# Delta rule's heads: a 16-column slab's TensorE passes set between those of the slab behind it

## The reference

```
proj = u @ w_in
dn_qkv, dn_z, dn_b, dn_a, ... = jnp.split(proj, idx, axis=-1)
qkv = jax.nn.silu(causal_depthwise_conv(dn_qkv, conv_w))
q, k, v = jnp.split(qkv, 3, axis=-1)          # q and k are then l2-normed by head
beta = jax.nn.sigmoid(dn_b)
g = -jnp.exp(a_log) * jax.nn.softplus(dn_a + dt_bias)
o_a = gated_delta_rule(q, k, v, g, beta)
```

## Time and profile before

| | |
|---|---|
| time, median of 3 runs | 3174.45 us (3172.67 to 3175.84) |
| profiled execution, its own time | 3191.96 us |
| its span, first to last instruction | 3190.7 us |
| mean granted clock of TensorE | 0.952 of full |
| PE busy | 3049.1 us (96%) |
| DVE, ACT, POOL busy | 2014.7, 1233.4, 340.1 us |

### The profile page before, as it was taken

One profiled execution on the slowest core, in us unless ns is written; L12 is line 12 of the kernel. 1 busy time (PEld: TensorE's weight loads), 2 busy tenths in 40 slices (PEclk: granted clock), 3 DMA queues, 4 the chain that ended last, 5 costly groups with the idle time before them and its releaser, 6 DMA issues.

```text
span 3190.7 us, 55249 instructions
## 1 busy us (share of the span) xinstructions
PE 3049.1 (96%) x23638; PEld 2868.9 (90%) x23638; DVE 2014.7 (63%) x2878; ACT 1233.4 (39%) x1633; POOL 340.1 (11%) x331
## 2 busy tenths in 40 slices
PE   7999998999998799998999999999999999999999
PEld 4888887999998677998999989889999998997998
DVE  4576586777786577677656854566565576446654
ACT  2222223545443133433544421445454443134643
POOL 5000001101010122002100020011020102000201
PEclk9999998999998799898998989999999999999999
DMA  7243244799996566797655612346576663232664
GB/s 262 95 151 127 89 156 116 204 258 270 262 280 196 160 210 201 202 257 215 180 164 151 168 54 67 100 131 180 169 197 168 168 160 92 65 96 69 191 168 129
DMA packets 746224, 524.76 MB, mean 164 GB/s; under 512 B 19242, under 2 KB 711660, under 8 KB 745852
## 3 DMA queue, kind: packets, MB, share of 16 engines
q1 hardware_dynamic: 741852, 516.18, 56.4%
q0 software_dynamic: 4128, 5.06, 0.5%
HBM read 520.07 MB, written 2.94 MB: 164 GB/s over the span
## 4 chain that ended last, share of the span: by engine, by line
PE 79%; DVE 9%; ACT 5%; issue 5%; DMA 2%; SPq 0%; POOL 0%; DVEq 0%; ACTq 0%; POOLq 0%
PE bank L478 21%; PE bank L479 20%; PE bank L480 20%; ACT weights_hi L448 3%; PE bank L1415 2%; PE bank L596 2%; DVE weights_lo L458 1%; DVE conv_out L2242 1%; PE bank L2407 1%; PE bank L820 1%; PE bank L2419 1%; PE bank L2415 1%; DMA side_weights<-in_ada_w 1%; PE bank L1420 1%; DVE side_sums_odd L565 1%
## 5 line engine op out<-in xcount | busy, mean ns | idle before, releaser
L458 DVE TENSOR_TENSOR weights_lo<-weights_raw,weights_hi 128x2048 fp32r<-128x2048 f32 (+3 forms) x414 | 853.9, 2063 | 375.7 <-ACT weights_hi L448 375.2
L448 ACT ACTIVATE weights_hi<-weights_raw 128x2048 fp32r<-128x2048 f32 (+3 forms) x414 | 709.4, 1714 | 695.5 <-PE bank L480 581.6
L478 PE MATMUL bank<-ffn_in_hi,weights_hi 128*128 128x256 f32 x1184 | 344.0, 291 | 25.6 <-DVE modulation L612 16.4
L479 PE MATMUL bank<-ffn_in_lo,weights_hi 128*128 128x256 f32 x1184 | 339.9, 287 | 0.0
L480 PE MATMUL bank<-ffn_in_hi,weights_lo 128*128 128x256 f32 x1184 | 339.6, 287 | 0.0
L478 PE MATMUL bank<-mix_in_hi,weights_hi 128*128 128x256 f32 x960 | 285.2, 297 | 6.2 <-DVE mix_in_lo L1926 3.7
L478 PE MATMUL bank<-mac_in_hi,weights_hi 128*128 128x256 f32 x1024 | 289.5, 283 | 1.5 <-DVE mac_prod L2025 1.0
L480 PE MATMUL bank<-mac_in_hi,weights_lo 128*128 128x256 f32 x1024 | 289.8, 283 | 0.0
L479 PE MATMUL bank<-mac_in_lo,weights_hi 128*128 128x256 f32 x1024 | 289.5, 283 | 0.0
L479 PE MATMUL bank<-mix_in_lo,weights_hi 128*128 128x256 f32 x960 | 277.4, 289 | 0.0
L480 PE MATMUL bank<-mix_in_hi,weights_lo 128*128 128x256 f32 x960 | 277.0, 289 | 0.0
(11 more groups left out here) (442 smaller groups left out, 7487.7 us busy)
## 6 DMA issues: line engine op xcount, KB each, us to landing
weights_raw<-in_ffn_w SPq DMA_DIRECT2D x132, 512.0 KB, 6.4
weights_raw<-in_w_in SPq DMA_DIRECT2D x120, 512.0 KB, 5.0
side_weights<-in_ada_w SPq DMA_DIRECT2D x85, 576.0 KB, 4.4
weights_raw<-in_ffn_wg SPq DMA_DIRECT2D x88, 512.0 KB, 4.0
weights_raw<-in_ffn_wu SPq DMA_DIRECT2D x88, 512.0 KB, 5.3
weights_raw<-in_ffn_wd SPq DMA_DIRECT2D x64, 704.0 KB, 4.6
weights_raw<-in_ffn_w SPq DMA_DIRECT2D x48, 704.0 KB, 6.7
side_weights_third<-in_ada_w SPq DMA_DIRECT2D x43, 576.0 KB, 4.5
```

Of the source, the lines that this page charges most:

```text
L448: k.s.activation(k.w_hi[s % HIGHS][:, 0:n], k.raw[s % RING][:, 0:n], ACT.Copy).then_inc(*k.hi.up())
L458: k.v.tensor_tensor(k.w_lo[s % RING][:, 0:n], k.raw[s % RING][:, 0:n], k.w_hi[s % HIGHS][:, 0:n].bitcast(F32), ALU.subtract).then_inc(*k.l ...
L478: k.te.matmul(out, l[0], r[0], start=first, stop=False)
L479: k.te.matmul(out, l[0], r[1], start=False, stop=False)
```

## The change

In `pe_heads` the narrow slab no longer has a stretch of its own. At n = 4 PE takes the slab and its bank, and goes on to n = 5. There it takes slab 5 and its banks too, and then issues by turns three passes of the narrow slab and three of slab 5, sixteen times: for each half c and each of 8 chunks. The narrow slab's `used` is raised by its last pass, three passes ahead of the end. The sums of squares move from behind a slab to ahead of the next one, with 3 in place of 2 in the condition, which leaves them where they were for all heads but head 1, whose sums now stand ahead of the narrow passes. No operation is added or removed, and no other engine's program is altered.

```diff
     for n in range(2 * DN_H + 1):
+        for hd in range(DN_H):
+            if qk_slab(hd) + 3 == n:
+                pe_qk_sums(k, hd)
         w = pe_slab(k)
         bank = pe_turn(k)
+        if n == BA_AT:
+            narrow = w, bank[0]
+            continue
         if n == 0:
...
-        elif n == BA_AT:
-            for tt in range(2):
-                m = token_major(k, bank[0][:, tt * 16:(tt + 1) * 16], w, 0, 16, u, tt * P)
+        elif n == BA_AT + 1:
+            for c in range(2):
+                for i in range(KD):
+                    x = passes(k, narrow[1][:, c * 16:(c + 1) * 16], [y[:, i, c * P:(c + 1) * P] for y in u],
+                               [y[:, i, 0:16] for y in narrow[0]], i == 0, i == KD - 1)
+                    if c == 1 and i == KD - 1:
+                        x.then_inc(*k.used.up())
+                    m = passes(k, bank[c][:, 0:T], [y[:, i, c * P:(c + 1) * P] for y in w], [y[:, i, :] for y in u],
+                               i == 0, i == KD - 1)
         else:
...
-        for hd in range(DN_H):
-            if qk_slab(hd) + 2 == n:
-                pe_qk_sums(k, hd)
```

More of the change, by code:

```diff
@@ L2136, in pe_heads @@
         m.then_inc(*k.used.up())
-        for hd in range(DN_H):
-            if qk_slab(hd) + 2 == n:
-                pe_qk_sums(k, hd)
     for hd in range(DN_H):
-        if qk_slab(hd) + 2 > 2 * DN_H:
+        if qk_slab(hd) + 3 > 2 * DN_H:
             m = pe_qk_sums(k, hd)
```

## The result

| | before | changed |
|---|---|---|
| median of the runs, side by side | 3175.14 us (3172.67 to 3183.09, 4 runs) | 3209.45 us (3205.31 to 3212.87, 4 runs) |
| profiled execution: its time, its span | 3191.96, 3190.7 us | 3205.31, 3204.0 us |

The change makes the kernel slower, 1.0112 times the time before, with a 95% interval of 1.0089 to 1.0134, which is 28 to 43 us. The changed kernel was timed a second time later, against a fresh set of runs of the kernel before, and gave 1.0091 [1.0066, 1.0116]. The forecast was 3205 us, 30.6 us more than before. Three executions of 9320 to 13764 us, two of the kernel before and one of a variant, were in the slow state and enter no ratio.

The account below looks back on a forecast made before the run. The chain on DVE and ACT behind the narrow slab's end was taken to bound the loop. 14.8 + 14.4 + 1.4 = 30.6 us on the median 3174.45 gave 3205 us, range 3198 to 3210 (about 0.68).

Parts of the forecast that it names:

- What bounds the stage: From the narrow slab's end to the last sums, the DVE and ACT chain paces the loop; any delay arrives there unshortened.
- Sums of head 1: Moved ahead of the narrow passes, they start without a wait and take 0.81 us at full clock.
- The moved wait: Ahead of the mixture PE waits for slab 5's banks, freed by DVE's copy L2272; it starts 3.1 us later than before.
- The mixed stretch: Alternating narrow and slab 5 passes run mostly at low clock, 19.0 us; narrow slab ends 14.8 and 14.4 us later.
- the lower bound: Mixed stretch if the clock falls only 3.05 us in: 28 fast passes, 65 slow ones, 17.0 us.
- Behind the stretch: DVE and ACT chain unchanged; PE stands ahead of slab 7 until about T + 11.6 us, costing nothing more.
- The end of the loop: Low clock in the filling slab after PE's wait for ACT in both layers; 1.4 us more, once.
- The sum and the base: Whole program: 30.6 us added to the runs' median of 3174.45 us gives 3205 us.
- Rival A: Clock holds in the mixed stretch, which takes 10.6 us; 13.8 us slower in all, 3188 us; chance 0.12.
- Rival B: Narrow passes vanish between wide ones in the mixed stretch; 3177 us, no change to be told; chance 0.05.
- Rival C: PE bounds the loop after all; 4.8 us saved twice, 3165 us; chance 0.04.
- Rival D: Clock rises within the mixed stretch, or falls in one layer only; about 3196 us; chance 0.06.

Follow-up runs that it names:

- gate_first_before: Kernel before, with ACT's Silu of the gate ahead of its weights_hi in every second slab: 3169.35 us, ratio 0.9984.
- wait_only: Changed kernel with the narrow slab in one piece again, unmixed, still behind the wait for slab 5's banks: 3190.43 us against 3173.06, ratio 1.0048.
- changed_again: The changed kernel, unaltered, timed and profiled a second time: 3207.67 us against 3181.73 for the kernel before, ratio 1.0091.
- own_bank_mixed: Changed kernel with the narrow slab in a bank of its own, so nothing waits ahead of the mixture: 3194.71 us, ratio 1.0065 to the kernel before.
- decay_split_mixed: own_bank_sums_behind plus ACT's activation of z ahead of its high part and the decay chain cut in two: 3160.65 us, ratio 0.9951 to the kernel before.
- own_bank_sums_behind: own_bank_mixed with the sums of head 1 moved behind slab 5: 3187.07 us against 3177.11 for the kernel before, ratio 1.0039.

## What the prediction had right, and which step failed

*What bounds the stage.* Right, to 0.03 us: copy to last sums takes 78.0 us in every kernel that keeps ACT's order. The 67.4 us from L2266 to the last sums are 1823.21 - 1755.82 = 67.39. Shortening that chain by another edit shortened the loop in the profile (gate_first_before). One sentence of it said too much: "no row of DVE or ACT between there and the end waits for PE". In the kernel before ACT did wait for PE once in this stretch:

```profile
1752.38 1.92 ACT L448 ACTIVATE weights_hi<-weights_raw 128x2048 fp32r<-128x2048 f32 x1 [1.53 <-PE bank L480]
```

In the changed kernel there is no such wait between the copy and the last sums, and the 78.0 us are the same, so this one was not on the chain.

*Sums of head 1.* Right: no wait ahead of them (1723.84 us). As to their cost, the prediction had only their 0.81 us; without the pause they may also decide whether the clock holds, which is not shown.

*The moved wait.* Right: start 3.15 and 3.14 us later than the narrow slab's before, 3.1 forecast, ended by the copy it named. wait_only shows this piece alone.

*The mixed stretch.* 19.0 us forecast; 1745.03 - 1726.99 = 18.04 and 2595.90 - 2576.07 = 19.83 us measured. T is 13.9 and 15.2 us later, forecast 14.8 and 14.4. In changed_again both mixtures took 19.84 us, and T was 15.7 and 15.2 us later. So in three mixtures of four no pass was fast, and "about seven passes still fast" is not what happened: the one other had some 20, not far from the 28 of the lower bound. That the 29.1 us of the first profile stand so close to the forecast's 29.2 is in part luck; the second profile has 30.9. What chose between the ends is when the clock falls, and that differs between executions.

*Behind the stretch.* Right: slab 7 starts 1756.72 - 1745.03 = 11.7 us behind T, after 3.38 us of waiting, and costs nothing.

*The end of the loop.* **This is the step that failed: the term was mis-sized.** I wrote "I expect it low in both: 15 passes of the filling slab at 0.212 in place of 0.119 are 1.4 us, once", taking the second layer's share as already paid before. It was 1.5 and 1.6 us, 3.1 in all, and in changed_again 1.5 and 1.6 again. The first layer went as forecast. In the second the low stretch grew, which the term had put at nothing: about 15 slow passes before, 27 now. The two stretches, before and now:

```profile
2653.30:2656.50 3.20, 3.20 (x18) 3.20 (x17) 2.82 (x6) 0.46 (x2) 0.00 (x0) 0.50 0.40 95
...
2675.40:2681.20 5.80, 5.80 (x28) 5.80 (x29) 4.54 (x7) 1.11 (x3) 0.00 (x0) 0.50 0.25 61
```

Before, the clock fell about 1 us after the filling slab had begun; now it is low from its first pass. Beside the 17.0 us of gate_first_before, the low clock cost 0.1 and 1.6 us before and 1.6 and 3.2 us now. With 3.1 the sum is 32.3, and the trace has 32.2 from slab 3 on. The wait for ACT is longer too (2.38 us for 1.95), but why the clock stayed low for longer no run settles: in own_bank_mixed a wait of 3.40 us cost 1.6 us, as 1.95 had done before.

*The sum and the base.* The two ratios are 36 [28, 43] and 29 [21, 37] us. The loops' 32 us lie in both. The median of the four runs is 4.4 us above the forecast: 1.7 of it is the term just named. Another 1.7 would be the mixtures, if most executions are like changed_again, whose 30.9 + 3.1 = 34.0 us come near the 34.3 between the two medians; that rests on two profiles. The rest is smaller than the scatter of the runs.

*Rival A*, the clock holds, is refuted for the change as it stands; without the wait it holds in some executions (T 6.9 us earlier than if it falls). *Rival B* is refuted: where the clock is full, the mixture takes 0.114 us a pass, narrow ones included, and no narrow pass is free. By the Trainium skill, page "TensorE: Matmul & The Clock Gate", section "Step-by-step: what each phase is for", a weight load overlaps the matmul ahead of it. The trace agrees (PE and PEld are both busy for 10.61 of 10.61 us), but nothing is left to win, since the loads already fill the time. *Rival C* needed the chain on DVE and ACT shorter, the start not to wait and the clock to hold. decay_split_mixed has all three, and it is faster. *Rival D* did not come: in the four mixtures of the changed kernel the clock was low to the end.

## What to carry to other kernels

Ask of a stage which single event of the busiest engine the others wait for, and what the edit does to the time of that event, not to the engine's work. Putting useful passes ahead of it delays everything that hangs on it, and a wait that moves with them loses whatever covered it. If the change is still wanted, first take the work that hangs on the event off the chain (here the decay), and give the moved piece resources of its own.

## What the hardware showed unexpectedly

The same mixture in the same program took 10.6 us at a granted clock of 1.00 in one execution and 17.4 us at 0.57 in another, with PE busy without a gap in both. Over the two mixtures of a run that is some 14 us, more than the whole of gate_first_before or own_bank_sums_behind by their ratios.

PE being busy was not enough to lift the clock: in the changed kernel it stayed at 0.50 for 15.5 us in which PE and PEld were both busy all of the time, half of the passes 256 columns wide. It was back at 1.00 behind them, in wide passes alone (1750 to 1753 us). Sixteen columns and 256 cost about the same at either level, 0.109 and 0.119 us at the high one and 0.21 at the low one, so narrow passes are paid for twice: by their own time, and by the clock of what runs behind them.
